# Forgetting attention: the key sums spread once into four PSUM banks, copied, masked and added by VectorE

## The chip, the core and the metric

The kernel runs on one core of a Trainium2 chip. TensorE multiplies into eight PSUM banks (bank 0 to bank 7), VectorE, ScalarE and GpSimd do the rest, SyncE starts most loads. Each engine has its own queue and works it off in order; they meet at semaphores. The metric is the device time of one execution in microseconds. Engine names in rows: PE is TensorE's matmul, PEld its weight load, DVE VectorE, ACT ScalarE, POOL GpSimd; a q behind a name is the engine's sequencer.

## The reference, cut to what matters

Two layers run one after the other on 256 tokens of 1024 features. Only one part of the first matters here, the attention with a forget gate:

```python
log_f = jax.nn.log_sigmoid(f_logit.astype(jnp.float32))        # 256 tokens x 8 heads
cum_f = jnp.cumsum(log_f, axis=1).transpose(0, 2, 1)
scale = dh ** -0.5                                             # dh = 64
for i in range(s // Q_BLOCK):                                  # blocks of 128 queries
    logits = jnp.einsum('bhqd,bhkd->bhqk', qb, kb).astype(jnp.float32) * scale
    logits = logits + cum_f[:, :, qs:qe, None] - cum_f[:, :, None, :qe]
    logits = jnp.where(causal[None, None], logits, NEG_INF)
    p = jax.nn.softmax(logits, axis=-1).astype(v.dtype)
    outs.append(jnp.einsum('bhqk,bhkd->bhqd', p, vb))
```

To the score of a query and a key, the running sum at the query is added and the running sum at the key subtracted, and later keys are masked. Beside this attention the layer has a windowed mean over tokens ("pooling mixer") and a short convolution of three taps; all three are multiplied by their rows of w_branch and by sigmoid gates.

## The kernel before

**Weights.** All weight matrices go through one ring of four slots, in 248 units of 512 KB (128 partitions x 1024 numbers). For unit u SyncE loads the slot, ScalarE rounds it into hi_ring (line 568), VectorE writes the rest into lo_ring (line 1104), and TensorE multiplies. A unit of the gates has twelve matmuls of 512 columns, in four triples of high x high, low x high, high x low (lines 2050 to 2052). Units 16 to 19 (MIX_B) are the second half of the mixers' inputs, units 20 to 43 the gates. `after(u)` on ScalarE and VectorE is the splitting of unit u + 4. Beside it VectorE adds up products for the modulation vectors (line 1136, "ada").

**Steps.** The attention is laid beside these units by hand. Step n is unit 16 + n, on every engine: `attention1(step)` of TensorE, ScalarE and VectorE, and on TensorE `beside1(step)`, which gives `beside(i)`, called after the i-th triple of a unit. `ATT1_AT = (5, 10, 15, 21)` are the steps at which the scores of the four head pairs are made: pair 0 in unit 21, pair 1 in unit 26, and so on. At step + 1 ScalarE takes the exponentials, at + 2 it normalizes, at + 5 TensorE turns the probabilities (`turn_prob`), at + 6 it multiplies them by the values (`attend`). ScalarE's copy of the turned probabilities is `take_both` (line 660).

**The forget gate.** VectorE sums up over the tokens (line 1401) and writes the running sums, times 8 and in two parts, to `key_sums` (rows cum_by_keys, line 1405), one partition a head and part. For the queries, `cumulative()` of step 1 turns them with two small matmuls into bank 6 (line 2287), and VectorE reads that bank into cum8 (rows cum_log_f, line 1412). For the keys, each score block gets a further matmul with the head picker as weights (line 2351), which adds the head's key sums to all 128 rows. A pair has four blocks: two heads times two query tiles, of 128 and of 256 keys. The four of a pair stand after the four triples of the unit; the scores (line 2338) stand after the first. VectorE then adds cum8 and a mask of 256 columns in one step a block (line 1272), the mask having been made by GpSimd at the start (lines 1918 and 1919).

**GpSimd** works in this order around there: it starts small loads, masks the second layer's gate weights w_s_T (line 1963), computes the pooling mixer's window sums (lines 1971 to 1988, tile 0 and then tile 1), writes the convolution's input (line 1997), and adds up the taps (line 2002) that ScalarE multiplies (line 776, steps 8 to 10).

**Banks.** `claim(b)` before a write waits for what `free[b]` names, the last reader of the bank. Units 16 to 19 write banks 0 to 3, units 20 to 23 banks 6 and 7, scores banks 4 and 5, the turned probabilities 6 and 7, the attended values 6.

Of the kernel before, what the change touches and what calls it, by code (L numbers as in the profile page):

```python
# [12 lines left out]
P = 128  # L13
# [18 lines left out]
DMA = 16  # L32
MIX_B_BANKS, Q2_BANKS = (0, 2), (2, 4)
# [228 lines left out]
class Signals:  # L262


    def __init__(self, new):
# [16 lines left out]
        self.ident_ok, self.mask_ok, self.dist_ok, self.consts_ok, self.wsT_ok, self.pad_zero = (  # L282
            new("ident_ok"), new("mask_ok"), new("dist_ok"), new("consts_ok"), new("wsT_ok"), new("pad_zero"))
# [54 lines left out]
class Memory:  # L338


    def __init__(self, nc, ctx):
# [48 lines left out]
        self.mask = sb("mask", [S])  # L390
# [45 lines left out]
        self.cnt16 = att[:, :].rearrange("p (a w) -> p a w", w=16)  # L436
        self.r_token = stat[:, 4:6]
# [118 lines left out]
def act_program(nc, t, m, s):  # L556
# [180 lines left out]
    def attention1(step):  # L737
        for g, at in enumerate(ATT1_AT):
            if step == at + 1:
                exponentials(s.att1, g, m.soft1[g])  # L740
            if step == at + 2:
                normalize(s.att1, g, m.soft1[g])
            if step == at + 4:
                take_both(s.att1, g, 6, m.turned1[g])
            if step == at + 5:
                attended_hi(s.att1, g, 6, g)
# [346 lines left out]
def dve_program(nc, m, s):  # L1093
# [170 lines left out]
    def take_scores(a, g, b0, b1, soft, forget):  # L1264

        dve.wait_ge(*a.scores.at(g + 1))
        mx, negmx, _ = m.pair_stats(g)
        for e, tt, c0, c1 in parts():
            src = bank[b1 if e else b0][:, c0:c1]
            keys = slice(P, S) if tt == 0 else slice(0, S)  # L1270
            if forget:
                ins = dve.scalar_tensor_tensor(out=soft[:, e, c0:c1], in0=src,
                                               scalar=m.cum8[:, tt, 2 * g + e:2 * g + e + 1], in1=m.mask[:, keys],
                                               op0=ALU.add, op1=ALU.add)
            else:
                slope = 2.0 ** (-8.0 * (2 * g + e + 1) / NH)
                ins = dve.scalar_tensor_tensor(out=soft[:, e, c0:c1], in0=m.dist[:, keys], scalar=8.0 * slope, in1=src,
                                               op0=ALU.mult, op1=ALU.add)
        ins.then_inc(a.logits.sem, 1)
        dve.wait_ge(*a.logits.at(g + 1))  # L1280
        for e, tt, c0, c1 in parts():
            i = 2 * e + tt
            ins = dve.tensor_reduce(mx[:, i:i + 1], soft[:, e, c0:c1], AX.X, ALU.max)
        own.then(ins)
        dve.tensor_scalar(negmx, mx, -0.125, None, ALU.mult).then_inc(a.max.sem, 1)
# [123 lines left out]
    def attention1(step):  # L1409
        if step == 1:  # L1410
            dve.wait_ge(s.cum_ps, 1)
            dve.tensor_scalar(m.cum8[:, :, :].rearrange("p a h -> p (a h)"), bank[6][:, 0:2 * NH], -1.0, None,
                              ALU.mult).then_inc(s.cum_out, 1)
            dve.wait_ge(s.cum_out, 1)
            dve.wait_ge(s.mask_ok, 1)
        for g, at in enumerate(ATT1_AT):
            if step == at:
                take_scores(s.att1, g, 4, 5, m.soft1[g], True)
            if step == at + 2:
                reciprocals(s.att1, g)  # L1420
# [437 lines left out]
def pool_program(nc, t, m, s):  # L1858
# [56 lines left out]
    def load_small(dst, src):  # L1915
        pool.dma_start(dst, src).then_inc(s.small_in, DMA)

    own.then(pool.memset(m.mask[:, :], 0.0))
    then_sem(pool.affine_select(out=m.mask[:, :], in_=m.mask[:, :], compare_op=ALU.is_ge, fill=8 * NEG, base=P,
                                pattern=[[-1, S]], channel_multiplier=1), s.mask_ok, 1)  # L1920
# [36 lines left out]
    for g in range(4):  # L1957
# [4 lines left out]
    pool.wait_ge(s.small_in, SMALL_LOADS * DMA)  # L1962
    then_sem(pool.affine_select(out=m.ws_T[:, :, :], in_=m.ws_T[:, :, :], compare_op=ALU.is_ge, fill=0.0, base=0,
                                pattern=[[0, 4], [1, P]], channel_multiplier=-1), s.wsT_ok, 1)


# [3 lines left out]
    for tile in range(2):  # L1970
# [14 lines left out]
        for rows, buf in ((slice(0, 64), low), (slice(64, P), src)):  # L1985
# [5 lines left out]
            else:  # L1991
                own.then(ins)

# [9 lines left out]
    then_sem(pool.tensor_tensor(y, y, mix[:, 4:6, :], ALU.mult), s.conv_ok, 1)  # L2003

# [32 lines left out]
def pe_program(nc, m, s):  # L2037
# [295 lines left out]
    def scores(a, g, banks, forget=False):  # L2333


        for e, tt, c0, c1 in parts():
            rows = slice(64 * e, 64 * e + 64)
            mm = pe.matmul(bank[banks[e]][:, c0:c1], m.qT[rows, g, tt * P:tt * P + P], m.kT[rows, g, 0:c1 - c0],  # L2338
                           start=tt == 0, stop=not forget, skip_group_check=True)
        if not forget:  # L2340
            scored(a, g, banks, mm)

    def scored(a, g, banks, mm):
        mm.then_inc(a.scores.sem, 1)
        free[banks[0]] = free[banks[1]] = a.logits.at(g + 1)

    def add_sums(a, g, banks, i):

        e, tt, c0, c1 = parts()[i]
        head = 2 * g + e  # L2350
        mm = pe.matmul(bank[banks[e]][:, c0:c1], m.pick[:, head:head + 1].to_broadcast([P, P]),
                       m.key_sums[:, 0:c1 - c0], start=False, stop=True, skip_group_check=True)
        if i == 3:
            scored(a, g, banks, mm)
# [23 lines left out]
    def beside1(step):  # L2378
# [8 lines left out]
        def beside(i):  # L2387
# [6 lines left out]
            if here is None:  # L2394
                return
            if i == 0:
                claim(4, 5)
                if here == 0:
                    pe.wait_ge(s.q_out, 2)
                    pe.wait_ge(s.k_out, 2)  # L2400
                    pe.wait_ge(s.key_sums, 1)
                    pe.wait_ge(s.pick_ok, 1)
                scores(s.att1, here, (4, 5), True)
            if i < 4:
                add_sums(s.att1, here, (4, 5), i)
# [17 lines left out]

    def attention1(step):
        if step == 1:
            cumulative()

# [504 lines left out]
```

## Time and profile before

| | |
|---|---|
| median of 3 runs | 773.0 us (772.85 to 773.22) |
| the profiled execution | 773.14 us |
| its span | 771.9 us |
| busy: TensorE, VectorE, ScalarE, GpSimd | 760.2, 582.1, 443.5, 76.4 us |
| granted TensorE clock | 0.999 of full speed |
| loads and stores | 161.29 MB, 208 GB/s from HBM |

The span runs from the first to the last instruction of the core; 1.2 us lie around it. The page gives busy times by engine and by line; the waits' list gives who waited for whom; a timeline gives instructions in order of time. Busy time of TensorE's matmuls is modelled at their ends, and one overlaps the next, so what a matmul costs is read from the distance of two starts, not from its duration.

### The profile page before, as it was taken

How to read it: one execution, taken by the hardware profiler on the slowest of the kernel's cores; microseconds unless marked ns; L12 is line 12 of the kernel's file. 1: busy time of each engine (PE TensorE's matmuls, PEld its weight loads, DVE VectorE, ACT ScalarE, POOL GpSimd, SP SyncE). 2: the span in 40 equal slices, each digit the busy share in tenths (PEclk: the TensorE clock that was granted, in tenths of full speed). 3: DMA queues.
4: the chain of work that ended last, by engine and by line, in shares of the span. 5: the costliest groups of instructions: out<-in, count | busy, mean ns of one | idle time of the engine just before them, and what ended most of it. 6: DMA issues, size and time to landing. Idle time of an engine off the chain costs nothing.

```text
span 771.9 us, 11259 instructions
## 1 busy us (share of the span) xinstructions
PE 760.2 (98%) x4342; PEld 656.4 (85%) x4342; DVE 582.1 (75%) x804; ACT 443.5 (57%) x666; POOL 76.4 (10%) x134
## 2 busy tenths in 40 slices
PE   6999999999999999999999999999999999999997
PEld 5998777888898888888899997789988888888885
DVE  5889999889896676686677998667757756665664
ACT  6567687865665444444474487567646644444452
POOL 5033930000200000000020001110001100000001
PEclk9999999999999999999999999999999999999999
DMA  9999988765466676856557554446434655666651
GB/s 323 367 284 327 363 306 310 255 196 167 134 204 227 213 260 204 299 186 203 181 154 238 160 173 137 138 163 219 137 110 136 216 191 193 190 194 190 190 165 55
DMA packets 84132, 161.29 MB, mean 209 GB/s; under 512 B 5408, under 2 KB 15968, under 8 KB 84080
## 3 DMA queue, kind: packets, MB, share of 16 engines
q1 hardware_dynamic: 82656, 157.31, 62.1%
q10 hardware_dynamic: 992, 2.78, 1.1%
q8 instruction: 34, 0.56, 0.3%
q0 software_dynamic: 432, 0.49, 0.3%
q14 instruction: 18, 0.15, 0.1%
HBM read 159.51 MB, written 1.05 MB: 208 GB/s over the span
## 4 chain that ended last, share of the span: by engine, by line
PE 95%; DVE 2%; DMA 1%; issue 1%; SPq 0%; POOL 0%; ACT 0%; DVEq 0%; POOLq 0%; ACTq 0%
PE bank L2050 18%; PE bank L2051 18%; PE bank L2052 18%; PE bank L2140 15%; PE bank L2143 8%; PE bank L2112 5%; PE bank L2063 2%; PE bank L2070 1%; PE bank L2065 1%; PE bank L2523 1%; PE bank L2193 1%; PE bank L2338 1%; DMA ada_ring<-in_w_ada 1%; PE bank L2361 1%; DVE ada_acc L1136 1%
## 5 line engine op out<-in xcount | busy, mean ns | idle before, releaser
L1104 DVE TENSOR_TENSOR lo_ring<-raw_ring,hi_ring 128x1024 fp32r<-128x1024 f32 x247 | 302.3, 1229 | 133.5 <-ACT hi_ring L568 132.8
L568 ACT CAST hi_ring<-raw_ring 128x1024 fp32r<-128x1024 f32 x248 | 259.8, 1052 | 241.8 <-PE bank L2052 127.1
L2050 PE MATMUL bank<-hi_ring,branch_hi 128*128 128x512 f32 x352 | 138.4, 393 | 0.0
L2051 PE MATMUL bank<-lo_ring,branch_hi 128*128 128x512 f32 x352 | 137.2, 390 | 0.0
L2052 PE MATMUL bank<-hi_ring,branch_lo 128*128 128x512 f32 x352 | 137.0, 389 | 0.0
L2140 PE MATMUL bank<-h_hi_lo,hi_ring 128*128 128x512 f32 x512 | 128.1, 392 | 0.0
L2140 PEld LDWEIGHTS bank<-h_hi_lo,hi_ring 128*128 128x128 f32 x512 | 92.9, 189 | 17.2
L2052 PEld LDWEIGHTS bank<-hi_ring,branch_lo 128*128 128x128 f32 x352 | 66.1, 188 | 14.0
L2050 PEld LDWEIGHTS bank<-hi_ring,branch_hi 128*128 128x128 f32 x352 | 66.2, 188 | 13.6 <-issue 0.6
L2051 PEld LDWEIGHTS bank<-lo_ring,branch_hi 128*128 128x128 f32 x352 | 66.2, 188 | 13.1 <-issue 0.2
L2143 PEld LDWEIGHTS bank<-h_hi_lo,lo_ring 128*128 128x128 f32 x512 | 69.8, 190 | 5.0
L2143 PE MATMUL bank<-h_hi_lo,lo_ring 128*128 128x256 f32 x512 | 71.4, 282 | 0.0
L2050 PE MATMUL bank<-hi_ring,h_hi_lo 128*128 128x512 f32 (+1 forms) x160 | 62.8, 392 | 0.0
L2052 PE MATMUL bank<-hi_ring,h_hi_lo 128*128 128x512 f32 (+1 forms) x160 | 60.8, 380 | 0.0
L2051 PE MATMUL bank<-lo_ring,h_hi_lo 128*128 128x512 f32 (+1 forms) x160 | 60.7, 380 | 0.0
L1890 POOL TENSOR_SCALAR stat<-stat 128x1 f32<-128x1 f32 x10 | 2.6, 259 | 429.3 <-ACT gates L632 429.3
L2050 PEld LDWEIGHTS bank<-hi_ring,h_hi_lo 128*128 128x128 f32 x160 | 30.1, 188 | 6.1 <-issue 1.2
L2052 PEld LDWEIGHTS bank<-hi_ring,h_hi_lo 128*128 128x128 f32 x160 | 30.1, 188 | 5.9
L2051 PEld LDWEIGHTS bank<-lo_ring,h_hi_lo 128*128 128x128 f32 x160 | 30.2, 189 | 4.6
L2112 PE MATMUL bank<-h_hi_lo,hi_ring 128*128 128x256 f32 x192 | 25.7, 284 | 0.0
L1653 DVE SCALAR_TENSOR_TENSOR mix<-pad_u,vector_columns,mix 128x256 f32<-128x256 f32 x60 | 25.2, 482 | 0.0
L2112 PEld LDWEIGHTS bank<-h_hi_lo,hi_ring 128*128 128x128 f32 x192 | 24.4, 192 | 0.5
(332 smaller groups left out, 1179.1 us busy)
## 6 DMA issues: line engine op xcount, KB each, us to landing
raw_ring<-in_w_ff SPq DMA_DIRECT2D x128, 512.0 KB, 3.6
raw_ring<-in_w_in SPq DMA_DIRECT2D x64, 512.0 KB, 4.9
raw_ring<-in_w_out SPq DMA_DIRECT2D x16, 512.0 KB, 3.4
raw_ring<-in_w_xkv SPq DMA_DIRECT2D x16, 512.0 KB, 3.5
mem_v<-in_w_ada SPq DMA_DIRECT2D x13, 512.0 KB, 5.6
mem_k<-in_w_ada SPq DMA_DIRECT2D x11, 512.0 KB, 5.7
ada_ring<-in_w_ada SPq DMA_DIRECT2D x8, 512.0 KB, 7.2
raw_ring<-in_w_branch SPq DMA_DIRECT2D x8, 512.0 KB, 3.3
```

The lines of the kernel that those rows point to most:

```text
L568: act.copy(m.hi[:, m.slot(u)], m.raw[:, m.slot(u)]).then_inc(s.hi_done, 1)
L1104: dve.tensor_tensor(m.lo[:, m.slot(u)], m.raw[:, m.slot(u)], as_f32(m.hi[:, m.slot(u)]), ALU.subtract).then_inc(s.lo_done, 1)
L1136: ins = dve.scalar_tensor_tensor(out=acc, in0=w, scalar=m.silu_c[:, kc:kc + 1], in1=acc, op0=ALU.mult, op1=ALU.add)
L1653: ins = dve.scalar_tensor_tensor(out=m.conv_y2[:, tile, :], in0=m.pad_u[:, tile, k:k + S], scalar=w, in1=m.conv_y2[:, tile, :], op0=ALU.mu ...
L2050: pe.matmul(out, a_hi, b_hi, start=start, stop=False, skip_group_check=True)
L2051: pe.matmul(out, a_hi, b_lo, start=False, stop=False, skip_group_check=True)
L2052: return pe.matmul(out, a_lo, b_hi, start=False, stop=stop, skip_group_check=True)
L2063: pe.matmul(out, m.hi[:, slot, k, fc], x_hi[:, k0 + k, :], start=first and k == 0 and f % 2 == 0, stop=False, skip_group_check=True)
L2065: pe.matmul(out, m.lo[:, slot, k, fc], x_hi[:, k0 + k, :], start=False, stop=False, skip_group_check=True)
L2112: mm = pe.matmul(out, w, x, start=start, stop=j == RING - 1 and i >= 20, skip_group_check=True)
L2140: pe.matmul(b, m.hi[:, slot, k, fc], x_both[:, k0 + k].rearrange("p a s -> p (a s)"), start=first and k == 0, stop=False, skip_group_check ...
L2143: mm = pe.matmul(b[:, 0:S], m.lo[:, slot, k, fc], x_both[:, k0 + k, 0, :], start=False, stop=last and k == UK - 1, skip_group_check=True)
```

## The change

The key sums no longer go through TensorE once a score block. `spread_sums()`, at step 1 right after `cumulative()`, multiplies the head picker by all 256 key sums for each of the eight heads, two heads to a bank, into banks 4, 5, 7 and 6. ScalarE copies the four banks into h_f32 (rows h_f), and GpSimd masks them in two selects of 8 heads x 128 keys: one from the first 128 keys into the second half of post_rows (the diagonal blocks of query tile 0), one in place on the second 128 keys (those of tile 1). VectorE's score step adds this buffer in the place of the mask, after waiting for both selects. The scores of a pair stand after the unit's first triple, or, where probabilities are turned in the same unit (units 26 and 31), after the second triple, right behind the turn. On GpSimd the making of the old mask is gone, the masking of w_s_T stands after the convolution, and the two selects stand in the window sums of tile 0, after the first half's two steps.

```diff
+KEY_BANKS = 4, 5, 7, 6
...
+        self.keys = self.rows[:, 1, :].rearrange("p (h c) -> p h c", c=P), self.h_f32
...
     def attention1(step):
+        if step == 1:
+            for n, b in enumerate(KEY_BANKS):
+                act.wait_ge(s.keys_ps, n + 1)
+                act.copy(pair(m.keys[1], 2 * n), bank[b][:, :]).then_inc(s.keys_done, 1)
...
-                ins = dve.scalar_tensor_tensor(out=soft[:, e, c0:c1], in0=src,
-                                               scalar=m.cum8[:, tt, 2 * g + e:2 * g + e + 1], in1=m.mask[:, keys],
-                                               op0=ALU.add, op1=ALU.add)
+                head = 2 * g + e
+                ins = dve.scalar_tensor_tensor(out=soft[:, e, c0:c1], in0=src, scalar=m.cum8[:, tt, head:head + 1],
+                                               in1=m.keys[tt][:, head, :], op0=ALU.add, op1=ALU.add)
...
             if step == at:
+                dve.wait_ge(s.keys_done, len(KEY_BANKS) + 2)
                 take_scores(s.att1, g, 4, 5, m.soft1[g], True)
...
-    own.then(pool.memset(m.mask[:, :], 0.0))
-    then_sem(pool.affine_select(out=m.mask[:, :], in_=m.mask[:, :], compare_op=ALU.is_ge, fill=8 * NEG, base=P,
-                                pattern=[[-1, S]], channel_multiplier=1), s.mask_ok, 1)
...
-    pool.wait_ge(s.small_in, SMALL_LOADS * DMA)
-    then_sem(pool.affine_select(out=m.ws_T[:, :, :], in_=m.ws_T[:, :, :], compare_op=ALU.is_ge, fill=0.0, base=0,
-                                pattern=[[0, 4], [1, P]], channel_multiplier=-1), s.wsT_ok, 1)
+    def mask_keys():
+        pool.wait_ge(s.keys_done, len(KEY_BANKS))
+        for i, dst in enumerate((m.keys[0], m.keys[1][:, :, P:S])):
+            then_sem(pool.affine_select(out=dst, in_=m.keys[1][:, :, i * P:i * P + P], compare_op=ALU.is_ge, fill=8 * NEG,
+                                        base=0, pattern=[[0, NH], [-1, P]], channel_multiplier=1), s.keys_done, len(KEY_BANKS) + i + 1)
...
+            if tile == 0 and buf is low:
+                mask_keys()
...
     then_sem(pool.tensor_tensor(y, y, mix[:, 4:6, :], ALU.mult), s.conv_ok, 1)
+    pool.wait_ge(s.small_in, SMALL_LOADS * DMA)
+    then_sem(pool.affine_select(out=m.ws_T[:, :, :], in_=m.ws_T[:, :, :], compare_op=ALU.is_ge, fill=0.0, base=0,
+                                pattern=[[0, 4], [1, P]], channel_multiplier=-1), s.wsT_ok, 1)
...
-            if i == 0:
+            if here is not None and i == (0 if turn is None else 1):
                 claim(4, 5)
...
-                scores(s.att1, here, (4, 5), True)
-            if i < 4:
-                add_sums(s.att1, here, (4, 5), i)
+                scores(s.att1, here, (4, 5))
...
+    def spread_sums():
+        pe.wait_ge(s.key_sums, 1)
+        pe.wait_ge(s.pick_ok, 1)
+        for n, b in enumerate(KEY_BANKS):
+            claim(b)
+            for e in range(2):
+                head = 2 * n + e
+                mm = pe.matmul(bank[b][:, e * S:e * S + S], m.pick[:, head:head + 1].to_broadcast([P, P]),
+                               m.key_sums[:, :], start=True, stop=True, skip_group_check=True)
+            mm.then_inc(s.keys_ps, 1)
+            free[b] = s.keys_done, n + 1
```

TensorE at the end of unit 17 (step 1), before: the last row of unit 17, `cumulative()`, and units 18 and 19.

```order
L2143 MATMUL bank<-h_hi_lo,lo_ring 128x256 x8
L2287 MATMUL bank<-ident,gates 128x8 [waits cum_rows,mixA_out]
L2287 MATMUL bank<-ident,gates 128x8
L2140 MATMUL bank<-h_hi_lo,hi_ring 128x512 [waits lo_done]
L2140 MATMUL bank<-h_hi_lo,hi_ring 128x512 x7
```

The same place after (cum_by_keys is key_sums, head_picker is pick; v_sum frees bank 5, mixA_out bank 7, cum_out bank 6):

```order
L2155 MATMUL bank<-h_hi_lo,lo_ring 128x256 x8
L2299 MATMUL bank<-ident,gates 128x8 [waits cum_rows,mixA_out]
L2299 MATMUL bank<-ident,gates 128x8
L2425 MATMUL bank<-cum_by_keys,head_picker 128x256 [waits fl_sum,pick_ok,cum_by_keys]
...
L2425 MATMUL bank<-cum_by_keys,head_picker 128x256 [waits v_sum]
...
L2425 MATMUL bank<-cum_by_keys,head_picker 128x256 [waits mixA_out]
...
L2425 MATMUL bank<-cum_by_keys,head_picker 128x256 [waits cum_out]
...
L2152 MATMUL bank<-h_hi_lo,hi_ring 128x512 [waits lo_done]
```

Eight matmuls stand there that did not, and the last two wait for VectorE to have read bank 6.

GpSimd from the load of w_s_T to the middle of the window sums, before:

```order
L1916 DMA w_s_T<-in_w_s_T 128x512 [waits fl_ps]
L1963 AFFINE_SELECT w_s_T<-w_s_T 128x512 [waits small_in]
L1971 MEMSET gates 128x16 [waits rcount_ok,mixA_out,wsT_ok]
...
L1988 TENSOR_TENSOR gates<-gates,mix 64x256 [waits pool_own]
L1986 TENSOR_TENSOR gates<-gates,pool_rcount 64x256 [waits pool_own]
```

and after:

```order
L1922 DMA w_s_T<-in_w_s_T 128x512 [waits fl_ps]
L1978 MEMSET gates 128x16 [waits rcount_ok,mixA_out]
...
L1995 TENSOR_TENSOR gates<-gates,mix 64x256 [waits pool_own]
L1971 AFFINE_SELECT post_rows<-h_f 128x1024 [waits keys_copied_then_masked,pool_own]
L1971 AFFINE_SELECT h_f<-h_f 128x8x128 [waits keys_copied_then_masked]
L1993 TENSOR_TENSOR gates<-gates,pool_rcount 64x256 [waits keys_copied_then_masked]
```

The masking of w_s_T is gone from ahead of the window sums, and the two new selects stand within them.

## Rows read from the trace of the kernel before

**Rows 1.** The page: span, and TensorE's busy time, share and instructions.

```profile
span 771.9 us, 11259 instructions
...
PE 760.2 (98%) x4342; PEld 656.4 (85%) x4342; DVE 582.1 (75%) x804; ACT 443.5 (57%) x666; POOL 76.4 (10%) x134
```

**Rows 2.** TensorE's waits, whole run: for whom, us, times, longest.

```profile
PE bank L2245 <- DMA x_residual<-in_x: 4.9, 1, 4.9
```

**Rows 3.** TensorE's timeline, unit 21 into 23: start, us, line, operation, out<-in, count.

```profile
80.85 0.39 PE L2052 MATMUL bank<-hi_ring,h_hi_lo 128*128 128x512 f32 x1
...
84.70 0.40 PE L2050 MATMUL bank<-hi_ring,h_hi_lo 128*128 128x512 f32 x1
...
87.46 0.39 PE L2050 MATMUL bank<-hi_ring,h_hi_lo 128*128 128x512 f32 x1
```

**Rows 4.** TensorE's timeline around one pair's scores in the second attention.

```profile
442.19 0.28 PE L2052 MATMUL bank<-memT_hi,lo_ring 128*128 128x256 f32 x1
442.40 0.93 PE L2338 MATMUL bank<-k_T,q_T 64*128 64x128 f32 x8
443.26 0.38 PE L2050 MATMUL bank<-memT_hi,hi_ring 128*128 128x256 f32 x1
443.48 0.28 PE L2051 MATMUL bank<-memT_lo,hi_ring 128*128 128x256 f32 x1
443.60 0.28 PE L2052 MATMUL bank<-memT_hi,lo_ring 128*128 128x256 f32 x1
```

**Rows 5.** TensorE's timeline, `cumulative()` and unit 18.

```profile
71.73 0.29 PE L2287 MATMUL bank<-ident,gates 8*128 8x8 f32 x2
71.94 2.14 PE L2140 MATMUL bank<-h_hi_lo,hi_ring 128*128 128x512 f32 x8
```

**Rows 6.** VectorE's timeline: mixer copy, key sums, splits, bank 6, scores, a later split.

```profile
67.83 0.67 DVE L1184 COPY mix<-bank 128x512 f32<-128x512 f32 x1
...
70.12 0.47 DVE L1405 SCALAR_TENSOR_TENSOR cum_by_keys<-gates,minus_one_in_low_rows 16x256 fp32r<-16x256 f32 x1
70.52 2.34 DVE L1104 TENSOR_TENSOR lo_ring<-raw_ring,hi_ring 128x1024 fp32r<-128x1024 f32 x2
72.79 0.15 DVE L1412 TENSOR_SCALAR cum_log_f<-bank 128x16 f32<-128x16 f32 x1
...
86.40 1.38 DVE L1272 SCALAR_TENSOR_TENSOR softmax<-bank,cum_log_f,mask 128x128 f32<-128x128 f32 x4
...
91.99 1.75 DVE L1104 TENSOR_TENSOR lo_ring<-raw_ring,hi_ring 128x1024 fp32r<-128x1024 f32 x1
```

**Rows 7.** ScalarE's timeline: a split, and two bank copies; brackets: idle before, releaser.

```profile
75.34 1.05 ACT L568 CAST hi_ring<-raw_ring 128x1024 fp32r<-128x1024 f32 x1 [1.90 <-DMA raw_ring<-in_w_in]
77.85 1.08 ACT L619 COPY mix<-bank 128x512 f32<-128x512 f32 x2 [1.46 <-PE bank L2143]
```

**Rows 8.** GpSimd's timeline: three selects, two steps of 64x256.

```profile
1.24 0.28 POOL L1909 TENSOR_SCALAR_AFFINE_SELECT ident<-ident 128x128 f32<-128x128 f32 x1 [0.24 <-POOL ident L1908]
...
9.07 0.40 POOL L1919 TENSOR_SCALAR_AFFINE_SELECT mask<-mask 128x256 f32<-128x256 f32 x1
...
70.24 3.13 POOL L1963 TENSOR_SCALAR_AFFINE_SELECT w_s_T<-w_s_T 128x512 f32<-128x512 f32 x1 [6.02 <-DMA w_s_T<-in_w_s_T]
...
79.98 0.73 POOL L1988 TENSOR_TENSOR gates<-gates,mix 64x256 f32<-64x256 f32 x1
80.79 1.59 POOL L1986 TENSOR_TENSOR gates<-gates,pool_rcount 64x256 f32<-64x256 f32 x1
```

**Rows 9.** ScalarE's timeline: first taps, copy of turned probabilities.

```profile
98.28 0.91 ACT L776 ACTIVATE gates<-pad_u,vector_columns 128x256 f32<-128x256 f32 x2 [0.30 <-POOL pad_u L1997]
...
100.04 0.79 ACT L660 COPY prob_T<-bank 128x768 f32<-128x768 f32 x1
```

**Rows 10.** TensorE's timeline: start of unit 26, first attended values.

```profile
95.62 0.39 PE L2050 MATMUL bank<-hi_ring,h_hi_lo 128*128 128x512 f32 x1
...
101.36 0.43 PE L2372 MATMUL bank<-prob_T,v_tok 128*64 128x128 f32 x2
```

More of the change, by code:

```diff
@@ L280, in __init__ @@
         self.out_done = new("out_done")
-        self.ident_ok, self.mask_ok, self.dist_ok, self.consts_ok, self.wsT_ok, self.pad_zero = (
-            new("ident_ok"), new("mask_ok"), new("dist_ok"), new("consts_ok"), new("wsT_ok"), new("pad_zero"))
+        self.ident_ok, self.dist_ok, self.consts_ok, self.wsT_ok, self.pad_zero = (
+            new("ident_ok"), new("dist_ok"), new("consts_ok"), new("wsT_ok"), new("pad_zero"))
+        self.keys_ps, self.keys_done = new("keys_ps"), new("keys_copied_then_masked")
         self.lo_first, self.first_cols_ps, self.first_cols = new("lo_first"), new("first_cols_ps"), new("first_cols")
@@ L389, in __init__ @@
         self.ones = sb("ones", [P])
-        self.mask = sb("mask", [S])
         self.dist = sb("neg_dist", [S])
@@ L1414, in attention1 @@
             dve.wait_ge(s.cum_out, 1)
-            dve.wait_ge(s.mask_ok, 1)
         for g, at in enumerate(ATT1_AT):
             if step == at:
+                dve.wait_ge(s.keys_done, len(KEY_BANKS) + 2)
                 take_scores(s.att1, g, 4, 5, m.soft1[g], True)
@@ L2331, in pe_program, with scores @@
     free[6] = free[7] = s.mixA_out, 2
-    def scores(a, g, banks, forget=False):
+    def scores(a, g, banks):
         for e, tt, c0, c1 in parts():
@@ L2338, in scores @@
             mm = pe.matmul(bank[banks[e]][:, c0:c1], m.qT[rows, g, tt * P:tt * P + P], m.kT[rows, g, 0:c1 - c0],
[L2339 to L2343, printed above, removed]
+                           start=tt == 0, stop=True, skip_group_check=True)
         mm.then_inc(a.scores.sem, 1)
         free[banks[0]] = free[banks[1]] = a.logits.at(g + 1)
[L2347 to L2354, printed above, removed]
     def turn_prob(a, g, banks, soft):
@@ L2393, in beside @@
                 turn_prob(s.att1, turn, (6, 7), m.soft1[turn])
-            if here is None:
-                return
-            if i == 0:
+            if here is not None and i == (0 if turn is None else 1):
                 claim(4, 5)
@@ L2400, in beside @@
                     pe.wait_ge(s.k_out, 2)
-                    pe.wait_ge(s.key_sums, 1)
-                    pe.wait_ge(s.pick_ok, 1)
-                scores(s.att1, here, (4, 5), True)
-            if i < 4:
-                add_sums(s.att1, here, (4, 5), i)
+                scores(s.att1, here, (4, 5))
         return beside
@@ L2426, in attention1 @@
             cumulative()
+            spread_sums()
     claim(0, 1, 2, 3)
```

## The prediction, made before the changed kernel ran

> **What bounds the kernel now.** I read the page first: TensorE is busy 98% of the span [rows 1]. The list of its waits for the whole run then shows one wait above 0.5 us, 4.9 us for the first load of x [rows 2]. So after the first microseconds TensorE never waits for another engine, and a microsecond put in or taken out of its queue moves the end by a microsecond, as long as no new wait comes up. Thirdly I read the timelines from 67 to 102 us, where the change lies, engine by engine. They show how much lead VectorE, ScalarE and GpSimd have there, and that is what decides whether a new wait comes up. The profiled execution took 773.14 us, with a span of 771.9 us; it lies 0.14 us above the median of the three runs, so differences may be added to either.
>
> **What TensorE loses in work.** Each of four head pairs has, inside one gate unit, four score matmuls and four matmuls that add the key sums. From the third matmul of unit 21 (80.85) to the start of unit 22 (84.70) pass 3.85 us; in them lie ten matmuls of the unit. A unit of twelve takes 87.46 - 84.70 = 2.76 us, 0.23 us each [rows 3], so ten are 2.29 us and 1.56 us are left for scores and sums. What scores cost alone is seen in the second attention, where none of the sums stand: from 442.19 to 443.48 pass 1.29 us with two 0.12 us matmuls in it, so 1.05 us [rows 4]. The sums are thus 0.51 us a pair, **-2.05 us** in all. In two of the four units the probabilities' transposes now stand directly ahead of the scores. One entry into another kind of matmul goes; before the scores it was 0.09 us (442.19 + 0.12 to 442.40 [rows 4]). I take 0.1 us each, **-0.2 us**, between 0 and 0.5 us for both.
>
> **What TensorE gains in work.** Eight 256-column matmuls after the two small transposes of the query sums. 256 columns go by at 0.12 us [rows 4], so **+0.96 us**, and 0 to 0.2 us for entering and leaving, taken as **+0.1 us**.
>
> **What TensorE gains in waits.** The sums by keys are ready: VectorE's last step on them ends at 70.59 [rows 6], the transposes run at 71.73 [rows 5]. Banks 4 and 5 were given free well before. The fourth bank is 6, into which the transposes have just written, and it comes free only when VectorE has read it. VectorE stands in two splits of weights until 72.79 and reads for 0.15 us, to 72.94 [rows 6]. In the kernel before, nobody waited for that. TensorE would now arrive after six matmuls, 71.94 + 0.72 = 72.7 [rows 5]: at least 0.25 us of wait. But VectorE will be later too. GpSimd no longer masks the gate weights here, a step that ended at 73.37 (70.24 + 3.13 [rows 8]), so its window sums start when their input is there, at 68.5 (67.83 + 0.67 [rows 6]), 4.9 us earlier, beside VectorE's key sums and two splits. A GpSimd step beside VectorE lengthens the split: 1.75 us where a pair of splits took 2.34 us, so 0.5 to 0.6 us [rows 6]. From 68.5 to 72.8 GpSimd gets through four or five steps, of which two to four meet a VectorE step: 0.5 to 2.2 us, I take 1.4 us. The read then ends at 74.35 and the wait is **+1.6 us** (0.25 to 2.5). Everything on TensorE stands behind this wait, and so do ScalarE's copies of the second mixer half, since they wait for TensorE's unit 19.
>
> **The sum:** -2.05 - 0.2 + 0.96 + 0.1 + 1.6 = **+0.4 us**, so 773.5 us for the profiled execution and 773.4 us by the median. With all bounds on the cheap side -2.05 - 0.5 + 0.96 + 0.25 = -1.3 us, on the dear side -2.05 + 0.96 + 0.2 + 2.5 = +1.6 us.
>
> **What lies beside other work.** ScalarE copies four banks. Two such copies take 1.08 us, four 2.2 us [rows 7]. ScalarE idles 1.90 us before its split at 75.34, waiting for a load [rows 7]; it is free from 73.4, so the copies run to 75.6 and push that split by 0.3 us. The next ScalarE step, the copies at 77.85, had waited for TensorE anyway. The fourth copy waits for the late bank 6, not for less than 75 us, which is the same time. Cost nothing; without this cover 2.2 us would fall on splits whose lead is 5 us. VectorE's four score steps a pair keep their shape and only read another buffer. The mask's two steps at 9 us go from an idle GpSimd. The masking of the gate weights moves behind the short convolution (about 107 us), where it may push VectorE by 0.5 us; the weights are wanted far later.
>
> **The two selects on GpSimd** are the step that the trace doesn't price. They process 1024 elements a partition each, in a two-level pattern of 8 heads by 128 keys. Low bound: one-level selects took 0.28 us for 128 and 0.40 us for 256 elements [rows 8], so 0.12 us for each further 128, 1.1 us for 1024 and 2.3 us for both. High bound: the gate weights' select, the only two-level one, took 3.13 us for 512 [rows 8]; taken per element this is 6.3 us for 1024 and 12.5 us for both. Which of them holds depends on whether the 3.13 us were work or waiting. That select ran beside the two VectorE splits, which ended at 72.86, and it ended 0.51 us later [rows 6, 8]. Extrapolated, an undisturbed 512-element select is 0.64 us. The same is seen with two steps of 64x256: 0.73 us where VectorE read PSUM, 1.59 us beside a split [rows 8]. I take it as waiting: each select 1.1 us of work and up to 2.5 us of waiting, together 2.3 to 7.2 us.
>
> What this hides behind: GpSimd reaches the selects at about 75 us and they start at 75.6, when the last copy is there. VectorE wants the masked sums at its first score step, at 86.40 now [rows 6] and about 2 us later then, since its work waits for TensorE's; 12.5 us would end at 88.1, so even they would just do. What follows on GpSimd is tighter. After the first half of tile 0 (80.71, end of the 0.73 us step [rows 8]) it needed 17.6 us until ScalarE could start its first convolution tap at 98.28, and ScalarE did wait for it, 0.30 us [rows 9]. Behind that tap on ScalarE stands the copy of the turned probabilities, ending at 100.83 [rows 9], and TensorE uses these at 101.36 [rows 10]. So there are 0.5 us to spare now. With t for both selects the tap starts at 75.6 + t + 17.6 = 93.2 + t, the copy ends 2.55 us later, and TensorE gets there at 101.36 + 1.5 = 102.9 (0.96 + 0.1 + 1.6 less two pairs' sums and 0.1). No wait up to t = 7 us.
>
> The Trainium skill ("SBUF — State Buffer", section Who interferes with whom) says that VectorE with two SBUF inputs and a GpSimd instruction share one port pair under an exclusive lock, held for a whole instruction. These two rows agree with it. By it the 3.13 us are mostly blocking and the sum stays at 773.4 us. The select's row agrees only half: by the rule it should have got in at the first split's start, at 70.6, and lengthened it, yet two splits ran in 2.34 us undisturbed. That speaks for slow work that takes no lock, and by that reading the sum is 779 us.
>
> **Rivals.** (1) **The selects are slow work** (slower). t = 12.5 us: the tap starts at 105.7, the copy ends at 108.3, TensorE waits 5.5 us at the first attended values, in unit 27. With +0.4 us that is 779.0 us. It decides from t = 7 us on, a microsecond for a microsecond. For it: the nearest row in form, and splits that weren't lengthened. Against it: the end 0.5 us after VectorE's splits, which would be chance. (2) **Bank 6 is there in time and the merged pieces save more** (faster): the wait is 0.25 us and entries save 0.5 us or slightly more, 771.6 to 771.8 us. For it: GpSimd's early steps fall beside 16-partition steps of 0.28 us too, which are hardly in its way. Against it: 1.75 us beside GpSimd. (3) **VectorE runs dry**: its lead was smallest at unit 26, whose split ended at 93.74 (91.99 + 1.75 [rows 6]) for a start at 95.62 [rows 10], 1.9 us; TensorE's savings of 0.6 us a pair and GpSimd's extra steps eat it. TensorE would then wait about 1.5 us, 775 us. Against it: the wait at bank 6 hands VectorE as much lead as it costs TensorE.
>
> **How the numbers follow.** A measurement of this kernel can tell about 0.2%, 1.5 us, from no change. Forecast 0.57 (own range 771.8 to 774.7 us; within 0.2% 0.50, faster 0.03, slower 0.04), rival 1 0.25 (slower, 775.5 to 779.5 us), rival 2 0.13 (faster 0.08, within 0.05), rival 3 0.05 (slower 0.04, within 0.01). Together faster 0.11, within 0.2% 0.56, slower 0.33. The range has to take in most of rival 1: 771.7 to 779.2 us.
>
> **What would show each step.** Unit 21 and its pieces from third matmul to next unit in 3.3 us instead of 3.85 us. A wait of TensorE for VectorE's small read of bank 6, 0.25 to 2.5 us, near 73 us. Two selects starting near 75.6 us: their durations decide between forecast and rival 1, with a ScalarE wait before its tap and a TensorE wait in unit 27 in the bad case. The forecast is wrong if TensorE waits anywhere else, above all for a split in units 22 to 31.

## The result, and the profile after

The changed kernel takes 774.77 us (median of 12 runs, 774.43 to 775.06), the kernel before 773.09 us in the same runs. The ratio is 1.0021 (95% interval 1.0013 to 1.0028): slower by 1.7 us. The profiled execution of the changed kernel took 774.58 us with a span of 773.3 us, 1.4 us more than before.

The page of the changed kernel, to be read against [rows 1]: TensorE has eight matmuls less and is busy 0.8 us less, while the span is 1.4 us longer. So TensorE waits somewhere for about 2 us.

```profile
span 773.3 us, 11254 instructions
...
PE 759.4 (98%) x4334; PEld 655.9 (85%) x4334; DVE 582.9 (75%) x804; ACT 445.1 (58%) x670; POOL 78.0 (10%) x134
```

TensorE's waits of the changed kernel, whole run (for whom, us, times, longest). Before, only the first stood above 0.5 us [rows 2].

```profile
PE bank L2257 <- DMA x_residual<-in_x: 5.1, 1, 5.1
PE bank L2360 <- ACT softmax L657: 1.1, 1, 1.1
PE bank L2307 <- DMA mem_k<-in_w_ada: 0.5, 1, 0.5
PE bank L2360 <- issue: 0.5, 1, 0.5
PE bank L2425 <- DVE cum_log_f L1418: 0.4, 1, 0.4
```

The 0.5 us for mem_k (line 2307) stand at 12 us, far ahead of the change, and the same wait came up in a kernel that differs from the kernel before in one late step only (experiment 10). Line 2360 is the turn of the probabilities: it waits 1.1 us in unit 26 for ScalarE's normalization, and 0.5 us in unit 36 for something that the view doesn't name. Line 2425 is the spreading of the key sums, waiting for bank 6.

TensorE's timeline of the changed kernel at step 1, answering to [rows 5], then in units 26 and 27, answering to [rows 10], then in unit 36:

```profile
71.78 0.28 PE L2299 MATMUL bank<-ident,gates 8*128 8x8 f32 x2
71.99 0.98 PE L2425 MATMUL bank<-cum_by_keys,head_picker 128*128 128x256 f32 x6
73.39 0.50 PE L2425 MATMUL bank<-cum_by_keys,head_picker 128*128 128x256 f32 x2 [0.41 <-DVE cum_log_f L1418]
...
96.74 0.39 PE L2062 MATMUL bank<-hi_ring,h_hi_lo 128*128 128x512 f32 x1
...
99.36 0.85 PE L2360 MATMUL bank<-ident,softmax 128*128 128x128 f32 x6 [1.10 <-ACT softmax L657]
...
103.26 0.43 PE L2371 MATMUL bank<-prob_T,v_tok 128*64 128x128 f32 x2
...
133.40 0.39 PE L2064 MATMUL bank<-hi_ring,h_hi_lo 128*128 128x512 f32 x1
134.27 0.85 PE L2360 MATMUL bank<-ident,softmax 128*128 128x128 f32 x6 [0.48 <-issue]
```

GpSimd's timeline of the changed kernel, answering to [rows 8]: the window sums, the two new selects, and the select of w_s_T at its new place. The last one is the same instruction that took 3.13 us before.

```profile
69.77 0.11 POOL L1978 MEMSET gates<- 128x16 f32 x1 [5.49 <-ACT mix L609]
...
70.79 2.96 POOL L1987 TENSOR_TENSOR gates<-pad_u 128x271 f32<-128x271 f32 x1
...
78.06 1.96 POOL L1971 TENSOR_SCALAR_AFFINE_SELECT post_rows<-h_f 128x1024 f32<-128x1024 f32 x1 [0.15 <-POOL gates L1995]
80.17 1.89 POOL L1971 TENSOR_SCALAR_AFFINE_SELECT h_f<-h_f 128x1024 f32<-128x1024 f32 x1
...
108.77 1.70 POOL L2014 TENSOR_SCALAR_AFFINE_SELECT w_s_T<-w_s_T 128x512 f32<-128x512 f32 x1
```

VectorE's timeline of the changed kernel, answering to [rows 6]: the key sums, two splits, the read of bank 6; the split of unit 22 and the product sum beside the first select; and the last read of bank 7 (line 1452).

```profile
70.48 0.50 DVE L1411 SCALAR_TENSOR_TENSOR cum_by_keys<-gates,minus_one_in_low_rows 16x256 fp32r<-16x256 f32 x1
70.90 2.34 DVE L1110 TENSOR_TENSOR lo_ring<-raw_ring,hi_ring 128x1024 fp32r<-128x1024 f32 x2
73.17 0.16 DVE L1418 TENSOR_SCALAR cum_log_f<-bank 128x16 f32<-128x16 f32 x1
...
77.84 1.22 DVE L1110 TENSOR_TENSOR lo_ring<-raw_ring,hi_ring 128x1024 fp32r<-128x1024 f32 x1 [1.36 <-ACT hi_ring L570]
78.99 2.12 DVE L1142 SCALAR_TENSOR_TENSOR ada_acc<-ada_ring,silu_c,ada_acc 128x1024 f32<-128x1024 f32 x1
...
133.29 0.88 DVE L1452 SCALAR_TENSOR_TENSOR branch_lo<-bank,vector_columns,branch_hi 128x256 fp32r<-128x256 f32 x2
```

ScalarE's timeline of the changed kernel, answering to [rows 7, 9]: the four copies, the split of unit 22, the normalization, the first tap.

```profile
73.49 2.05 ACT L743 COPY h_f<-bank 128x512 f32<-128x512 f32 x4
76.76 1.05 ACT L570 CAST hi_ring<-raw_ring 128x1024 fp32r<-128x1024 f32 x1 [1.23 <-PE bank L2155]
...
97.72 1.49 ACT L657 ACTIVATE softmax<-softmax,softmax_stats 128x128 f32<-128x128 f32 x4 [1.06 <-DVE softmax_stats L1296]
...
100.05 0.91 ACT L782 ACTIVATE gates<-pad_u,vector_columns 128x256 f32<-128x256 f32 x2
```

**Where the time is.** From the timelines I took, for each unit, TensorE's first matmul and the end of VectorE's split, and subtracted those of the kernel before. Positive is later.

| unit | TensorE later, us | VectorE's split later, us | what happened on TensorE |
|---|---|---|---|
| 20 | 1.65 | 0.38 | key sums spread, bank 6 waited for |
| 22 | 1.16 | 1.35 | sums of pair 0 gone (-0.49) |
| 26 | 1.12 | 2.17 | |
| 27 | 1.91 | 2.71 | sums of pair 1 gone, turn waits |
| 32 | 1.42 | 2.05 | sums of pair 2 gone (-0.49) |
| 36 | 1.44 | 2.04 | |
| 37 | 2.04 | 2.05 | turn waits |
| 38 | 1.58 | 2.04 | sums of pair 3 gone (-0.46) |
| 50 | 1.56 | 1.56 | |

VectorE is 2.05 us late from unit 31's split on. Not all of that is the change's: 0.35 us of it stand already at the split of unit 14, at 58 us, ahead of everything that was changed here but the mask's two steps at 9 us. There the profiled executions of all these kernels differ by -0.11 to 0.50 us from that of the kernel before, 0.13 us in experiment 10, where the mask's steps are kept. TensorE, which gains 0.5 us at each pair, runs into that lateness twice, and in unit 37 it is exactly as late as VectorE. After unit 38 TensorE's lateness stays within 0.03 us up to unit 50.

### The profile page after: what moved, and what is told of

The parts are those of the page before. It is cut to its first block, busy times and chain, and to the rows that moved or that the text cites. A ratio compares the mean times of both kernels' runs of the same rounds, so it can differ in the third digit from the quotient of the medians.

```text
span 773.3 us, 11254 instructions
## 1 busy us (share of the span) xinstructions
PE 759.4 (98%) x4334; PEld 655.9 (85%) x4334; DVE 582.9 (75%) x804; ACT 445.1 (58%) x670; POOL 78.0 (10%) x134
## 4 chain that ended last, share of the span: by engine, by line
PE 89%; DVE 6%; issue 2%; DMA 1%; ACT 1%; SPq 1%; POOL 0%; DVEq 0%; ACTq 0%; POOLq 0%
PE bank L2062 17%; PE bank L2063 17%; PE bank L2064 17%; PE bank L2152 14%; PE bank L2155 8%; PE bank L2124 3%; DVE lo_ring L1110 2%; PE bank L2075 2%; PE bank L2077 1%; PE bank L2082 1%; PE bank L2530 1%; DVE ada_acc L1142 1%; PE bank L2205 1%; DMA mem_k<-in_w_ada 1%; PE bank L2350 1%
```

## The experiments

Theory A: the changed kernel makes VectorE 2.05 us late, and TensorE's two waits in units 26 and 36 are this lateness, showing where TensorE needs results of VectorE and ScalarE that have little to spare. Theory B: each wait has a cause of its own, the one in unit 26 the place of the turn. Theory C: VectorE is late only because TensorE is. Each kernel ran beside the kernel before on the same chip (773.1 to 773.2 us). The changed kernel was not run again beside them, so its 774.77 us is compared across runs in which the kernel before differs by 0.1 us. The ratio to the kernel before has an interval of 0.0009 either way in each experiment, 0.7 us; differences of 0.3 us between two of the kernels lie within it.

**Experiment 1: the turn and the scores behind it later in the unit.**

```diff
-            if i == 1 and turn is not None:
+            if turn is not None and i == (1 if here is None else 3):
...
-            if here is not None and i == (0 if turn is None else 1):
+            if here is not None and i == (0 if turn is None else 3):
```

> The changed kernel with one thing moved: in units 26 and 31 the turn of the probabilities and the scores behind it stand after the fourth triple, not after the second. Theory A (VectorE's chain): in the changed kernel VectorE runs 2.05 us later than before from unit 31's split on and TensorE only 1.1 to 1.9 us, so TensorE's waits (1.1 us ahead of the turn in unit 26, 0.5 us ahead of the one in unit 36) are the same lateness showing at two places. Then the wait in unit 26 goes, 0.5 to 0.7 us come up at the attended values in unit 27, the wait in unit 36 grows by what TensorE gained (to 1 to 1.5 us), and the time stays at 774.8 us (774.5 to 774.9). Theory B (the place of the turn): the wait in unit 26 comes only from the turn being called 1.2 us earlier than before, ahead of the scores; then 1.1 us go and the time is 773.7 us.

Measured 774.75 us, as theory A has it; theory B wanted 773.7 us. TensorE's waits in this kernel, whole run, two rows:

```profile
PE bank L2360 <- issue: 1.1, 1, 1.1
PE bank L2371 <- ACT prob_T L662: 0.7, 1, 0.7
```

The wait in unit 26 is gone. 0.7 us came up at the attended values in unit 27, and the wait in unit 36 grew from 0.5 to 1.1 us. At unit 36 TensorE was only 0.72 us later than before, at unit 37 it was 1.97 us later, with VectorE's split at 1.98 us. The gain was made and given back. So theory B is wrong on the time, but not on the place: moving the turn alone removed the wait in unit 26.

**Experiment 2: no selects.**

```diff
-            if tile == 0 and buf is low:
-                mask_keys()
...
-                                               in1=m.keys[tt][:, head, :], op0=ALU.add, op1=ALU.add)
+                                               in1=m.keys[1][:, head, 0:c1 - c0], op0=ALU.add, op1=ALU.add)
...
-                dve.wait_ge(s.keys_done, len(KEY_BANKS) + 2)
+                dve.wait_ge(s.keys_done, len(KEY_BANKS))
```

> The changed kernel without the two selects on GpSimd: VectorE waits for ScalarE's four copies and adds the unmasked key sums to both query tiles, so the causal mask is left out. Theory A: the selects push VectorE by 0.6 to 0.8 us while they run beside it (one split and one product sum of 2.12 and 1.73 us instead of 1.28 and 1.22 us), so VectorE's lateness falls from 2.05 to about 1.4 us, the wait in unit 26 to about 0.6 us, and the time to 774.1 us. Rival C (VectorE is late only because TensorE is): the selects cost nothing, 774.8 us.

Measured 773.76 us, 1.0 us below the changed kernel, more than theory A expected. VectorE's lateness at unit 36 fell from 2.04 to 0.46 us. That is more than the 0.6 to 0.8 us read off two instructions; GpSimd's whole chain behind the selects also ends earlier (the convolution's input at 94.67 us instead of 98.74) and meets other steps of VectorE. Up to 0.37 us of the 1.6 us are no effect of the selects, since this execution lacks the lateness at unit 14. Experiments 7 and 9 give a second reading of the same step, 1.1 us (1.87 us against 0.78 us at unit 36). TensorE's wait in unit 36 is gone. The one in unit 26 is still 0.8 us, and VectorE's reciprocals, for which that turn's normalization waits, are still 1.53 us later than before, instead of 2.17 us. In the kernel before, in the changed one and in this one:

```profile
95.35 0.16 DVE L1290 RECIPROCAL softmax_stats<-softmax_stats 128x4 f32<-128x4 f32 x1
...
97.52 0.17 DVE L1296 RECIPROCAL softmax_stats<-softmax_stats 128x4 f32<-128x4 f32 x1
...
96.88 0.16 DVE L1296 RECIPROCAL softmax_stats<-softmax_stats 128x4 f32<-128x4 f32 x1
```

Theory C, by which the selects cost nothing, falls. But the selects make most of the lateness at unit 36, and only a part of that at unit 26.

**Experiment 3: the spreading one step later.**

ScalarE's program, and then TensorE's:

```diff
-        if step == 1:
+        if step == 2:
             for n, b in enumerate(KEY_BANKS):
...
             cumulative()
+        if step == 2:
             spread_sums()
```

> The changed kernel with the eight matmuls of the key sums, and ScalarE's four copies, one step later (after unit 18 instead of after unit 17). The 0.4 to 0.6 us wait for bank 6 goes, and ScalarE's split of unit 22, which waits for the end of unit 18, is no longer 1.4 us later. Theory A: VectorE's lateness falls from 2.05 to about 1.5 us and the time to 774.2 us. Rival (the lateness is made by the selects and the copies only, wherever they stand): 774.8 us, with the bank 6 wait gone and a longer wait in unit 26.

Measured 774.43 us, between the two expectations, and at 0.3 us below the changed kernel not clear of noise. The wait for bank 6 is gone, and TensorE is 1.06 us later at unit 20 instead of 1.65 (0.14 us of that ahead of the change). But VectorE's lateness fell only from 2.05 to 1.83 us, and TensorE's wait in unit 26 grew to 1.5 us. ScalarE's split of unit 22 was on time again (0.11 us early), and VectorE's was 1.11 us late there all the same. So VectorE's lateness stays wherever TensorE's spreading stands; with experiment 2, most of it at unit 36 is the selects' doing.

**Experiment 4: bank 7 read earlier.** The three ScalarE steps on the pooling mixer's product of step 17 stand ahead of the normalization, and VectorE's steps on it ahead of the split of unit 37 (ScalarE's program, and then VectorE's; mixers_high() is the three steps, and VectorE's two steps are moved unchanged):

```diff
                 after(GATES + i)
+                if i == 13:
+                    mixers_high()
                 attention1(RING + i)
...
             attention1(RING + i)
+            if i == 13:
+                dve.wait_ge(s.mixers_hi, 1)
...
             after(GATES + i)
```

> The changed kernel with the reading of bank 7 (pooling mixer's product, step 17) moved ahead of the normalization on ScalarE and ahead of the split of unit 37 on VectorE, so that bank 7 is free about 2 us earlier. If the 0.5 us wait ahead of the turn in unit 36 is for bank 7, as theory A says, it goes and the time is 774.2 us, the 1.1 us wait in unit 26 staying. If it is for the probabilities (a rival), it stays and the time is 774.8 us.

Measured 774.10 us, as expected. The gain of 0.7 us is at the edge of the interval; the traces bear it out, with TensorE 1.53 us late at unit 37 instead of 2.04 us. VectorE's steps on bank 7 in this kernel now begin at 131.08 us instead of 133.29, and behind them stands the split:

```profile
131.08 0.84 DVE L1448 SCALAR_TENSOR_TENSOR branch_lo<-bank,vector_columns,branch_hi 128x256 fp32r<-128x256 f32 x2
131.84 0.68 DVE L1453 TENSOR_TENSOR branch_lo<-gates,branch_hi 128x512 fp32r<-128x512 f32 x1
132.44 1.21 DVE L1114 TENSOR_TENSOR lo_ring<-raw_ring,hi_ring 128x1024 fp32r<-128x1024 f32 x1
```

That settles which resource the unnamed wait in unit 36 was for. The end of VectorE's read, 134.17 us in the changed kernel, lies 0.1 us ahead of the turn at 134.27, and in the kernel before the same read ended 0.1 us ahead of the turn at 132.22, with TensorE arriving at 132.18. There the release came just in time and cost next to nothing.

```profile
132.22 0.85 PE L2361 MATMUL bank<-ident,softmax 128*128 128x128 f32 x6
...
131.24 0.88 DVE L1446 SCALAR_TENSOR_TENSOR branch_lo<-bank,vector_columns,branch_hi 128x256 fp32r<-128x256 f32 x2
```

(Timelines of the kernel before, TensorE and VectorE.)

**Experiment 5: the moves of 1 and 4 together.**

> Both moves together: turn and scores after the fourth triple in units 26 and 31, and bank 7 read earlier. Theory A (VectorE's lateness shows as TensorE waits only where TensorE needs its results): the first alone left 774.75 us because the wait came back in unit 36; with bank 7 early it can't come back there, so both gains add up: 1.3 us below the changed kernel, 773.5 us, with one wait of 0.7 us left at the attended values in unit 27. Rival (the time is simply set by VectorE, which is as late as before): 774.1 us, as with bank 7 alone, and a new wait for a split in units 36 to 44.

Measured 773.18 us, 0.3 us better than expected, and level with the kernel before (ratio 0.9998, 0.9989 to 1.0007). Alone the move of experiment 1 was worth 0.0 us and that of 4 0.7 us, together they are worth 1.6 us. The rival, that VectorE sets the time everywhere, falls: its splits are as late as ever (1.93 us at unit 36) and TensorE doesn't wait for them.

**Experiment 6: the same, with the spreading one step later.**

> The same, and the eight matmuls of the key sums with ScalarE's copies one step later. Theory A: TensorE saves the 0.5 us wait for bank 6, but gets it back at the attended values in unit 27, which depend on ScalarE and VectorE; these gain 0.2 us only. 773.3 us. If the bank 6 saving comes through whole: 773.0 us.

Measured 773.19 us, nothing gained. The bank 6 wait is gone, and the wait at the attended values in unit 27 is 0.8 us instead of 0.7 us.

**Experiment 7: the same, and the first attended values late.**

```diff
-            if turned is not None and i == (1 if turned == 2 else 0):
+            if turned is not None and i == (1 if turned == 2 else 3 if turned == 0 else 0):
```

> The same, and the first pair's attended values after the fourth triple of unit 27 instead of the first. Then no wait of TensorE for the attention's probabilities is left, and what remains is the bare exchange of work: 1.9 us less for sums, 1.0 to 1.1 us more for spreading. Theory A: 772.4 us (below the kernel before by 0.8 us), if VectorE's splits of units 30, 31 and 36 still come in time; their leads shrink to 0.3 us or less, and each 0.1 us below none costs as much.

Measured 773.02 us (ratio to before 0.9995, 0.9986 to 1.0004). That is 0.6 us above the expectation, and not to be told from the kernel before. At unit 36 TensorE was 0.18 us ahead of the kernel before; then the turn in unit 36, no longer held up by bank 7, had to wait for the probabilities:

```profile
PE bank L2364 <- ACT softmax L657: 0.3, 1, 0.3
```

**Experiment 8: the select of w_s_T back in its old place.**

```diff
     load_small(m.ws_T[:, :, :], t["w_s_T"])
+    pool.wait_ge(s.small_in, SMALL_LOADS * DMA)
+    then_sem(pool.affine_select(out=m.ws_T[:, :, :], in_=m.ws_T[:, :, :], compare_op=ALU.is_ge, fill=0.0, base=0,
+                                pattern=[[0, 4], [1, P]], channel_multiplier=-1), s.wsT_ok, 1)
...
-    pool.wait_ge(s.small_in, SMALL_LOADS * DMA)
-    then_sem(pool.affine_select(out=m.ws_T[:, :, :], in_=m.ws_T[:, :, :], compare_op=ALU.is_ge, fill=0.0, base=0,
-                                pattern=[[0, 4], [1, P]], channel_multiplier=-1), s.wsT_ok, 1)
```

> The changed kernel with the select of the second layer's gate weights back in its old place, ahead of GpSimd's window sums. GpSimd's chain then starts at about 73.5 us instead of 69.8, the two new selects at about 81.5, and the convolution's input, 18.7 us after the first select's start in the changed kernel, comes at 101 us instead of 98.7. ScalarE wants it at 100.1. Theory (the threshold worked out in the prediction): ScalarE waits 1 us ahead of its first tap, TensorE 1 us at the attended values in unit 27, and the time is 775.2 us or, where the wait of unit 36 swallows it, 774.8. If GpSimd's early start is what pushes VectorE, the time falls instead, to 774.3 us.

Measured 775.07 us, 0.3 us above the changed kernel, which is within the noise, and near one of the expected values, but not for the expected reason. GpSimd's timeline of this kernel:

```profile
70.38 0.67 POOL L1966 TENSOR_SCALAR_AFFINE_SELECT w_s_T<-w_s_T 128x512 f32<-128x512 f32 x1 [5.91 <-DMA w_s_T<-in_w_s_T]
...
71.46 2.40 POOL L1983 COPY pad_u<-mix 128x256 f32<-128x256 f32 x1
```

The select took 0.67 us here, since it got in before the two splits, and the copy behind it waited for them instead. The convolution's input came only 0.8 us later (99.53 against 98.74 us), not 2.3 us, and ScalarE did not wait for it ahead of the first tap. The select lengthened VectorE's key-sum step from 0.50 to 0.74 us, and VectorE's lateness at unit 36 rose from 2.04 to 2.47 us. The threshold of 7 us for the selects, worked out in the prediction, was not tested by this.

**Experiment 9: experiment 7 without the selects.**

> The kernel with all four moves (turn and scores after the fourth triple, bank 7 early, key sums one step later, first attended values late) and without GpSimd's two selects, so the causal mask is left out. Theory A: what is left of TensorE's waits in that kernel, about 0.7 us for probabilities and splits, comes from VectorE's lateness of 1.2 to 1.9 us, which the selects and their collisions make. Without them VectorE is late by no more than 0.5 us, TensorE does not wait from unit 20 to unit 43, and the time is 772.3 us, 0.7 us below the kernel with all four moves: the bare exchange of 16 small matmuls for 8. If VectorE's lateness comes from TensorE's spreading, the time stays at 773.0 us.

Measured 772.17 us (ratio to before 0.9988, 0.9979 to 0.9997), as expected. VectorE's lateness at unit 36 was 0.78 us, where at most 0.5 us was expected, so the selects are not all of it. The list of TensorE's waits names none between units 20 and 43, and TensorE is 1.12 us ahead of the kernel before at unit 50. That is the bare exchange of 16 small matmuls for 8, for which the prediction's terms without the wait give -1.19 us. Against experiment 7 the selects cost 0.85 us even after everything has been arranged around them (0.8 us with each taken against the kernel before on its own chip).

**Experiment 10: the kernel before with bank 7 read earlier, a control.**

> The kernel before with the reading of bank 7 moved earlier as in the fourth experiment, a control. There TensorE doesn't wait ahead of the turn in unit 36, so nothing is to be gained: 773.1 to 773.2 us, ratio 1.000. Were the move worth something by itself, the 0.6 us that it gave in the changed kernel would not be that kernel's lateness, and this run would come out at 772.6 us.

Measured 773.13 us, ratio 1.0000 (0.9991 to 1.0009). The move is worth nothing by itself. What it gave in the changed kernel was that kernel's own lateness.

## Why the prediction was right or wrong

The range of 771.7 to 779.2 us held the time, and in part by luck: it was stretched upwards for rival 1, which was wrong. The forecast of 773.4 us was 1.4 us too low; 774.77 us lies just above its own range of 771.8 to 774.7 us. It lies next to the 775 us of rival 3, which had a chance of 0.05 and the right engine, but a wait for splits that never came. The chance of 0.56 was on a change within 0.2%, and the measured one is just above that. Two errors also went against each other: the wait at bank 6 was put 0.9 us too high, while the waits in units 26 and 36 were put at nothing. Counted like all terms by the distances of starts they are 1.3 and 0.6 us (the turns began at 99.36 and 134.27, and the matmul ahead of each ended its 0.23 us at 98.10 and 133.63).

**Sums taken off TensorE: right.** Predicted -0.51 us a pair; measured -0.49, -0.49 and -0.46 us at the three pairs where no wait hides it. The saving of 0.1 us for the scores directly behind the turn did not show: unit 31, which has it, also gained 0.49 us. With the turn after the fourth triple (experiment 1) units 26 and 31 gained 0.62 us each.

**Spreading: right.** Predicted 1.06 us without a wait. With the spreading one step later, where it had no wait, TensorE was 1.06 us later at unit 20, but 0.14 us of that were there before it, so the spreading cost 0.92 us. That the two figures are equal is chance.

**The wait for bank 6: the mechanism was right, the size wrong.** Predicted 1.6 us, within 0.25 to 2.5; measured 0.41 us in the list of waits, and 0.68 us as the prediction counted it, from 71.99 + 0.72 to 73.39. The term that failed is the push of 1.4 us that GpSimd's earlier window sums were to give VectorE. VectorE read bank 6 0.38 us later than before, and 0.36 us of that it was already late at the key sums, by the difference that stands there since unit 14. The window sums began at 69.77 us, not at 68.5: they waited for ScalarE's half of the mixer's copy (5.49 us of idle time, ended by ACT mix L609), and the prediction had looked at VectorE's half only. The two splits ran in 2.34 us, undisturbed as in [rows 6], and it was GpSimd that waited: its 271-column sum took 2.96 us.

**The selects: right on what they are, wrong on what they cost.** Rival 1 had them as slow work of 12.5 us. They took 1.96 and 1.89 us, and the w_s_T select took 0.67, 1.70 and 3.13 us in three kernels: it was waiting, and 0.64 us was the right extrapolation. The prediction then asked only whether they would end in time. They did, and ScalarE did not wait for the convolution. The first stood beside a product sum of 2.12 us and the second beside a split of 1.73 us, which take 1.28 and 1.22 us undisturbed; but in the kernel before, beside window sums, the same two steps took 1.66 and 1.38 us, so the direct loss is 0.8 us. Over all that follows, the experiments put the selects at 1.1 to 1.6 us of VectorE's time at unit 36. The prediction gave no term for it.

**The Trainium skill**'s rule of the shared port pair ("SBUF — State Buffer", section Who interferes with whom) agrees with the durations here, on both sides: GpSimd's steps end about as long after a VectorE step as they take alone, and VectorE's next step is longer. The objection in the prediction, that a GpSimd step should get in between two splits, stands: with three different GpSimd steps (a select, a sum, a copy) it did not, at this one place. Why is left open.

**The forecast itself** failed on its condition: "The forecast is wrong if TensorE waits anywhere else". It waited 1.1 us in unit 26 and 0.5 us in unit 36. Two steps of the working led there. First, moving the scores behind the turn was booked as a gain of 0.1 us an entry. It also calls the turn 1.2 us earlier in the unit, ahead of the scores and one sum. Unit 26 is the one that begins in [rows 10]. ScalarE's normalization and the turn there, in the timelines of the kernel before:

```profile
95.55 1.50 ACT L655 ACTIVATE softmax<-softmax,softmax_stats 128x128 f32<-128x128 f32 x4 [0.28 <-DVE softmax_stats L1290]
...
98.17 0.81 PE L2361 MATMUL bank<-ident,softmax 128*128 128x128 f32 x6
```

The probabilities were ready at 97.05, 1.1 us ahead of the turn. The earlier call used up that lead alone, and VectorE's lateness came on top. Secondly, rival 3 looked at the leads of the splits only. Those held (0.83 us were left at unit 26). What had the shortest lead were results of the attention and a bank's release. Rival 3 also said that the wait at bank 6 hands VectorE as much lead as it costs TensorE. It did not: ScalarE's split of unit 22, which waited for a load before, waited 1.23 us for TensorE's unit 18, so that VectorE stood idle for 1.36 us and was pushed together with TensorE, by the spreading and its wait.

## What to carry to other kernels

Work taken off the bounding engine comes through only up to the shortest lead of everything that it needs from the others, and that is not only the stream of operands: look up each product it consumes and each buffer it claims again, and write down how long each had been ready. When a wait is removed and the time stays, compare the engines' start times unit by unit with those of the old kernel. An engine that reaches exactly the lateness of another one shows where the gain went, and two repairs that are worth nothing and a little by themselves can be worth 1.6 us together.

## What the runs showed of the hardware

A GpSimd step of 0.67 us took 3.13 us when it was called while VectorE had two splits to go, and VectorE's two splits, back to back, took 2.34 us in every kernel at this place, whatever GpSimd had waiting (a select, a 271-column sum, a copy of 2.40 us). Between a split and a product sum GpSimd did get in, and the product sum took 1.66 to 2.12 us at the places shown here instead of 1.28 us. I had not expected the difference between these two boundaries, and no run explains it.
